# The last MLP chunk of a two-layer hybrid decoder: weight sums of two products built in a dead buffer, and the seven products in another order

## The chip, the cores and the metric

The kernel runs on one core of a Trainium2 chip. The metric is the device time of one execution in microseconds (us), lower is better. TensorE (PE) multiplies, VectorE (DVE), ScalarE (ACT) and GpSimd (POOL) work on elements, SyncE (SP) and GpSimd issue most DMA transfers. Each engine runs its own program in order; semaphores tie them together.

## The reference

Two layers, each with two token mixers merged by gates and then an MLP, on a sequence of 512 tokens and a width of 1024, all in float32. The change touches the MLP alone:

```
D_MODEL = 1024
SEQ = 512
DEPTH = 2
D_FF = 4 * D_MODEL
...
    h2 = rmsnorm(x, g_ffn)
    x = x + jnp.square(jax.nn.relu(h2 @ w_up)) @ w_down
```

## The kernel before

**Float32 in three passes.** Each float32 operand is split in a high part (a cast) and a low part (operand minus high part), and each product is three matmuls: high by high, high by low, low by high. ScalarE makes `w_hi`, DVE makes `w_lo`, both in two halves of 1024 columns; the same for the activations, `a_hi` and `a_lo`, of 128 x 1024 elements.

**The MLP by chunks.** The hidden width of 4096 is cut in `CH` = 4 chunks of 1024. For each chunk c, four up units `("U", c, u)` make the squared ReLU in the buffer `us[c % 2]`, and a down step multiplies it (512 x 1024) by 1024 x 1024 of `w_down`. The down step is done with seven products of halves in place of eight (Strassen's method in Winograd's form), numbered 1 to 7. Each product is a half of the tokens by a half of the chunk by a half of the output: 24 matmuls of 128 x 128 by 128 x 512 into two banks of PSUM. `M_SEQ` is the order of all units of the MLP; up units of the next chunk stand between the down products of a chunk, but the seven of the last chunk (`DOWN_LAST`, order 1 2 5 3 6 7 4) stand alone.

**Weight operands of the products.** With w00, w01, w10, w11 for the four quarters (h, m) of the chunk's `w_down`, product 1 uses w00, 5 uses w00+w01, 6 uses w00+w01+w11, 4 uses w00+w01+w11+w10, 3 uses w11, 7 uses w11+w01, and 2 uses w10. The sums are made by DMA: `sum_slot` (SP, L645) loads a quarter of 1 MB plain into `gh[slot]`, and `add_quarter` (GpSimd, L1114) adds another quarter to it with an accumulating DMA. Of the two buffers `gh`, one holds in turn the operands of 1, 5, 6, 4 (three adds) and the other those of 3, 7 (one add); which is which changes with the chunk. In the last chunk slot 1 has 1, 5, 6, 4 and slot 0 has 3, 7. Each add waits (`lo_done`) until DVE has read the operand that it overwrites. Product 2 reads w10 from the buffer `w_raw`, which all other weights pass through too (`load`, L475); a load waits until DVE's `w_lo` has read what was there.

**Activation operands.** Products 1, 2, 4 read a quarter of `us`, the others a sum: `sum_of` on DVE, in the chain 5, 6, 3 (each from the one before), and 7 by itself, in two buffers (`hn` and `sq`). `a_high` and `a_low` make the parts, in three sets that rotate.

**Order on the engines.** A weight set (two of them, rotating) is written once the product two before has been done (`mm_done`); so ScalarE's `weights_high` and DVE's `weights_low` work one unit ahead, in the order of `M_SEQ`, and an operand that isn't there yet holds up all that follow on ScalarE and DVE. TensorE starts a product when `a_ready`, the first half of `lo_done` and the eviction of the bank it needs (`acc_done`, `down_ready`) are there. Products 6, 7 and 4 are added in PSUM onto the bank that 1 opened, 3 onto that of 5; after each product DVE adds or subtracts the bank to the accumulators (`evict`), two of which are `acc[0]` and `tables`. In the last chunk all products are `halved`: the first 256 x 512 bank is finished, then the second (`down_halves`, `evict_half`), and each has its own eviction.

In layer 0 the last product is followed by transposes and the next layer's norm, in layer 1 by the final norm (`f_squares`, `f_scaled`) and the output. Both layers run the same down steps.

The functions that the change touches, with what calls them:

## Time and profile before

| | us |
|---|---|
| median of 3 runs | 1888.55 (1887.93 to 1889.95) |
| the profiled execution | 1888.48 |
| its span | 1886.4 |
| PE busy in the span | 1865.5 (99%) |
| DVE busy | 1255.6 (67%) |
| ACT busy | 837.2 (44%) |
| POOL busy | 129.4 (7%) |

The profile is of one execution. The span goes from its first to its last instruction. PE busy is modelled from the starts of pipelined matmuls; a matmul of 512 columns is shown with 0.39 us, but the next one starts 0.227 us after it, and this pace is what counts. Busy shares are means over the whole span; a gap on an engine is read in the timeline, where a row shows how long the engine had been idle and who released it. In the granted clock 1.00 is full speed (2.4 GHz). Layer 0's MLP ends near 941, layer 1's near 1879.

### The profile page before, as it was taken

To read this page: it belongs to the slowest core of one execution; us is meant where nothing else is said; L and a number is where in the kernel's file an instruction comes from. 1 tells how busy PE (TensorE), PEld (TensorE's weight loads), DVE (VectorE), ACT (ScalarE), POOL (GpSimd) and SP (SyncE) were. 2 spreads that over 40 slices of the span, in tenths; PEclk is the share of its full clock that TensorE was granted. 3 is DMA by queue.
4 is the path that set the end of the run, shared out by engine and by line. 5 is a ranking of instruction groups with operands and counts; after the bars stand their busy time and mean duration, and the time that the engine had idled before them with its cause. 6 is when DMAs were issued, how large, how long until landed. Compare 5 with 4: busy or idle time off the path is not lost.

```text
span 1886.4 us, 22990 instructions
## 1 busy us (share of the span) xinstructions
PE 1865.5 (99%) x9064; PEld 1549.7 (82%) x9064; DVE 1255.6 (67%) x1858; ACT 837.2 (44%) x1234; POOL 129.4 (7%) x104
## 2 busy tenths in 40 slices
PE   9999999999999999999899999999999999999997
PEld 7888888887888888888788888888878888888886
DVE  5356778767456666767863568788665575676777
ACT  7325465464223333434472255554632233344344
POOL 0001111100000000000000112111000000000100
PEclk9999999999999999999999999999999999999999
DMA  4543233333333465564626333233243334655655
GB/s 146 200 159 120 83 89 118 90 93 104 120 101 114 132 134 136 150 136 125 145 88 240 96 104 104 77 118 104 68 146 101 101 112 113 141 148 134 134 147 121
DMA packets 208235, 230.64 MB, mean 122 GB/s; under 512 B 13440, under 2 KB 160640, under 8 KB 207360
## 3 DMA queue, kind: packets, MB, share of 16 engines
q1 hardware_dynamic: 190512, 194.74, 32.7%
q0 software_dynamic: 16896, 33.56, 10.5%
q8 instruction: 72, 1.18, 0.2%
q10 hardware_dynamic: 720, 0.87, 0.1%
q14 instruction: 35, 0.29, 0.0%
HBM read 215.38 MB, written 13.77 MB: 121 GB/s over the span
## 4 chain that ended last, share of the span: by engine, by line
PE 85%; issue 6%; DVE 4%; DMA 3%; ACT 2%; POOL 0%; SPq 0%; POOLq 0%; ACTq 0%; DVEq 0%
PE pj L1816 19%; PE pj L1818 19%; PE pj L1817 19%; DMA gh<-in_w_down 2%; PE yr L2122 1%; PE yr L2124 1%; PE yr L2126 1%; DVE w_lo L1140 1%; PE pt L2122 1%; PE pt L2124 1%; PE pt L2126 1%; PE sc L2122 1%; PE sc L2124 1%; PE sc L2126 1%; PE yr L1923 1%
## 5 line engine op out<-in xcount | busy, mean ns | idle before, releaser
L1816 PE MATMUL pj<-h_hi,w_hi 128*128 128x512 f32 x1408 | 554.4, 394 | 1.0 <-DVE sA L1515 1.0
L1818 PE MATMUL pj<-h_hi,w_lo 128*128 128x512 f32 x1408 | 548.5, 390 | 0.0
L1817 PE MATMUL pj<-h_lo,w_hi 128*128 128x512 f32 x1408 | 548.3, 389 | 0.0
L1140 DVE TENSOR_TENSOR w_lo<-w_raw,w_hi 128x1024 fp32r<-128x1024 f32 x279 | 329.9, 1220 | 115.1 <-ACT w_hi L687 113.6
L687 ACT CAST w_hi<-w_raw 128x1024 fp32r<-128x1024 f32 x276 | 278.6, 1049 | 270.5 <-PE pj L1818 56.9
L1816 PEld LDWEIGHTS pj<-h_hi,w_hi 128*128 128x128 f32 x1408 | 264.4, 188 | 59.0 <-issue 1.9
L1818 PEld LDWEIGHTS pj<-h_hi,w_lo 128*128 128x128 f32 x1408 | 264.3, 188 | 56.0
L1817 PEld LDWEIGHTS pj<-h_lo,w_hi 128*128 128x128 f32 x1408 | 264.5, 188 | 53.9 <-issue 0.5
L697 ACT CAST w_hi<-gh 128x1024 fp32r<-128x1024 f32 x96 | 96.0, 1050 | 118.2 <-DMA gh<-in_w_down 50.5
L1107 POOL TENSOR_TENSOR rcos<-rot,tables 128x512 f32<-128x512 f32 x64 | 87.6, 1370 | 692.4 <-ACT rot L808 633.8
L1140 DVE TENSOR_TENSOR w_lo<-gh,w_hi 128x1024 fp32r<-128x1024 f32 x96 | 113.1, 1219 | 14.2 <-ACT w_hi L697 14.0
L975 ACT ACTIVATE relu<-pj 128x512 f32<-128x512 f32 x64 | 38.2, 597 | 189.6 <-PE pj L1818 189.6
L1581 DVE TENSOR_TENSOR u<-relu,rstd_all 128x512 f32<-128x512 f32 x64 | 44.0, 688 | 105.5 <-ACT relu L975 105.5
L1114 POOL DMA_DIRECT2D gh<-in_w_down x32 | 41.2, 1286 | 1038.4 <-DVE w_lo L1140 1038.4
L808 ACT COPY rot<-pj 128x512 f32<-128x512 f32 x48 | 27.9, 582 | 110.5 <-PE pj L1818 64.5
L2122 PE MATMUL sc<-w_hi,a_hi 128*128 128x512 f32 x160 | 63.3, 396 | 5.7 <-DVE a_lo L1623 3.4
L1288 DVE TENSOR_TENSOR swp<-swp,tables 128x512 f32<-128x512 f32 x64 | 65.4, 1022 | 4.4 <-ACT swp L812 2.7
L2126 PE MATMUL sc<-w_hi,a_lo 128*128 128x512 f32 x160 | 63.0, 394 | 0.0
L2124 PE MATMUL sc<-w_lo,a_hi 128*128 128x512 f32 x160 | 62.9, 393 | 0.0
L2122 PE MATMUL yr<-w_hi,a_hi 128*128 128x512 f32 x160 | 62.2, 389 | 0.0
L2124 PE MATMUL yr<-w_lo,a_hi 128*128 128x512 f32 x160 | 62.2, 389 | 0.0
L2126 PE MATMUL yr<-w_hi,a_lo 128*128 128x512 f32 x160 | 62.2, 389 | 0.0
(339 smaller groups left out, 3102.4 us busy)
## 6 DMA issues: line engine op xcount, KB each, us to landing
w_raw<-in_w_in SPq DMA_DIRECT2D x151, 512.0 KB, 4.7
w_raw<-in_w_up SPq DMA_DIRECT2D x64, 512.0 KB, 4.9
gh<-in_w_down POOLq DMA_DIRECT2D x32, 1024.0 KB, 8.7
gh<-in_w_down SPq DMA_DIRECT2D x16, 1024.0 KB, 5.1
w_raw<-in_w_b SPq DMA_DIRECT2D x16, 512.0 KB, 3.9
w_raw<-in_w_o SPq DMA_DIRECT2D x16, 512.0 KB, 3.9
w_raw<-in_w_down SPq DMA_DIRECT2D x16, 512.0 KB, 4.5
x_scratch<-x SPq DMA_DIRECT2D x2, 2048.0 KB, 10.1
```

What stands on the lines that cost most here:

```text
L687: nc.scalar.copy(w_hi[s][:, c], raw[:, c]).then_inc(hi_done, 1)
L697: nc.scalar.copy(w_hi[n % 2][:, h], gh[slot][:, h]).then_inc(hi_done, 1)
L1107: nc.gpsimd.tensor_tensor(rcos[:], rot[:], cosA if u < 3 else cosR, ALU.mult).then_inc(rot_cos, 1)
L1140: nc.vector.tensor_tensor(w_lo[s][:, c], src[:, c], w_hi[s][:, c], ALU.subtract).then_inc(lo_done, 1)
L1288: nc.vector.tensor_tensor(swp[:], swp[:], sinA if u < GROUPS else sinR, ALU.mult).then_inc(rot_sin, 1)
L1581: nc.vector.tensor_tensor(to, relu[:, o, :], rstd_all[:], ALU.mult).then_inc(relu_scaled, 1)
L1816: nc.tensor.matmul(out, w_hi[s][:, wc], acts[0], start=first, stop=False)
L1817: nc.tensor.matmul(out, w_hi[s][:, wc], acts[1], start=False, stop=False)
L1818: return nc.tensor.matmul(out, w_lo[s][:, wc], acts[0], start=False, stop=last)
L2122: nc.tensor.matmul(out, hi[:, k, t], w_hi[s][:, w], start=opens and k == 0, stop=False, skip_group_check=not opens)
L2124: nc.tensor.matmul(out, hi[:, k, t], w_lo[s][:, w], start=False, stop=False, skip_group_check=not opens)
L2126: return nc.tensor.matmul(out, lo[:, k, t], w_hi[s][:, w], start=False, stop=k == 3, skip_group_check=not opens)
```

## The change

Four things change, all in the last chunk (c = 3) of each layer:

1. The order of the seven products becomes 1 5 2 6 3 7 4, and the activation parts are made one product ahead in that order (`LAST_AHEAD`).
2. Product 1 reads w00 through `w_raw` (`plain`), with a load of its own on SP. `gh[1]` is still loaded with w00, but w01 is added at once, for product 5, and then w11 for product 6; `gh[0]` holds w11 for product 3 alone.
3. The operands of products 7 and 4 are built in `spares`, the two halves of `us[0]`, which held chunk 2's activations and is dead once `a_low` of (2,4) has read it. SP waits for that (`a_ready`) and loads w11 for 7 and w00 for 4; GpSimd adds one quarter for 7 and three for 4, each of these after the one before has landed.
4. Products 1, 5, 2, 6 and 3 are done whole and evicted whole; only 7 and 4 are still in halves.

GpSimd's last adds of layer 1 stand in its queue like this before (`gh_95` is slot 0, `gh_96` slot 1; `gh_96 x2` are the adds for products 5 and 6, the two after it those for 7 and 4):

```order
93 L1114 DMA gh_95<-in_w_down 128x4x512 [waits sum_in0,lo_done] x2
94 L1114 DMA gh_96<-in_w_down 128x4x512 [waits sum_in1,lo_done]
95 L1114 DMA gh_95<-in_w_down 128x4x512 [waits sum_in0,lo_done]
96 L1114 DMA gh_96<-in_w_down 128x4x512 [waits sum_in1,lo_done] x2
97 L1114 DMA gh_95<-in_w_down 128x4x512 [waits sum_in0,lo_done]
98 L1114 DMA gh_96<-in_w_down 128x4x512 [waits sum_in1,lo_done]
```

and now (`u_86` is `us[0]`):

```order
97 L1136 DMA gh_95<-in_w_down 128x4x512 [waits sum_in0,lo_done]
98 L1136 DMA gh_96<-in_w_down 128x4x512 [waits sum_in1]
99 L1144 DMA u_86<-in_w_down 128x4x512 [waits spare_in4]
100 L1144 DMA u_86<-in_w_down 128x4x512 [waits spare_in7]
101 L1144 DMA u_86<-in_w_down 128x4x512 [waits spare_added4] x2
102 L1136 DMA gh_96<-in_w_down 128x4x512 [waits sum_in1,lo_done]
```

The add for product 5 (row 98) no longer waits for `lo_done`; the four adds to the spares stand between it and the add for product 6 (row 102).

SP's last loads of weights in layer 1, before:

```order
191 L475 DMA w_raw<-in_w_up 128x4x256 [waits lo_done] x6
192 L645 DMA gh_96<-in_w_down 128x4x512 [waits lo_done]
193 L475 DMA w_raw<-in_w_down 128x2x512 [waits lo_done] x2
194 L645 DMA gh_95<-in_w_down 128x4x512 [waits lo_done]
195 L475 DMA w_raw<-in_w_down 128x2x512 [waits lo_done] x2
```

and now:

```order
193 L486 DMA w_raw<-in_w_up 128x4x256 [waits lo_done] x6
194 L656 DMA gh_96<-in_w_down 128x4x512 [waits lo_done]
195 L486 DMA w_raw<-in_w_down 128x2x512 [waits lo_done] x4
196 L679 DMA u_86<-in_w_down 128x4x512 [waits a_ready]
197 L679 DMA u_86<-in_w_down 128x4x512
198 L656 DMA gh_95<-in_w_down 128x4x512 [waits lo_done]
199 L486 DMA w_raw<-in_w_down 128x2x512 [waits lo_done] x2
```

Product 1's load (two of the x4) and the two loads of the spares are new, ahead of slot 0's load and of product 2's.

The diff, without the shorter pieces that only pass on the new order or the new test of `halved`:

```diff
-    DOWN_LAST = (1, 2, 5, 3, 6, 7, 4)
+    DOWN_LAST = (1, 5, 2, 6, 3, 7, 4)
+    LAST_AHEAD = {1: 2, 5: 6, 2: 3, 6: 7, 3: 4}
...
+    def plain(c, i):
+        return i == 2 or (c, i) == (CH - 1, 1)
+
     def by_raw(j):
-        return j < M0 or M_SEQ[j - M0][0] == "U" or M_SEQ[j - M0][2] == 2
+        return j < M0 or M_SEQ[j - M0][0] == "U" or plain(*M_SEQ[j - M0][1:])
...
-    def halved(c):
-        return c == CH - 1
+    def halved(c, i):
+        return c == CH - 1 and i in (7, 4)
...
+        spare = us[(CH - 2) % 2]
+        spares = {7: spare[:, 0:4, :].rearrange("p k c -> p (k c)"), 4: spare[:, 4:8, :].rearrange("p k c -> p (k c)")}
...
-                    load(m_unit(l, "D", c, 2), quarter(c))
+                    load(m_unit(l, "D", c, 2), quarter(c, 1))
+                    if c == CH - 2:
+                        load(m_unit(l, "D", c + 1, 1), quarter(c + 1, 0))
+                        sp.wait_ge(a_ready, l * LD + d_no(c, 4) + 1)
+                        for i, src in ((7, w_down_q[l, c + 1, 1, 1]), (4, w_down_q[l, c + 1, 0, 0])):
+                            sp.dma_start(spares[i].rearrange("p (k c) -> p k c", k=4), src).then_inc(spare_in[i], 16)
...
             def hi_sum(l, c, i, n):
+                if c == CH - 1 and i in (7, 4):
+                    act.wait_ge(spare_added[i], (l + 1) * 16 * {7: 1, 4: 3}[i])
+                    for h in HALVES:
+                        nc.scalar.copy(w_hi[n % 2][:, h], spares[i][:, h]).then_inc(hi_done, 1)
+                    return
...
                 def add_quarter(c, behind, as_sum, h, m):
                     slot = slot_of(l, c, as_sum)
-                    pool.wait_ge(lo_done, m_unit(l, "D", c, behind) * 2 + 2 + UNIT_CREDIT)
+                    if not plain(c, behind):
+                        pool.wait_ge(lo_done, m_unit(l, "D", c, behind) * 2 + 2 + UNIT_CREDIT)
                     pool.wait_ge(sum_in[slot], (l * CH + c) * 16 + 16)
...
+                def add_spare(i, n, h, m):
+                    if n == 0:
+                        pool.wait_ge(spare_in[i], l * 16 + 16)
+                    else:
+                        pool.wait_ge(spare_added[i], (l * 3 + n) * 16)
+                    nc.gpsimd.dma_start(spares[i].rearrange("p (k c) -> p k c", k=4), w_down_q[l, CH - 1, h, m],
+                                        accum_op=ALU.add).then_inc(spare_added[i], 16)
+
-                for c in range(CH):
+                for c in range(CH - 1):
                     add_quarter(c, 1, True, 0, 1)
                     add_quarter(c, 5, True, 1, 1)
                     add_quarter(c, 3, False, 0, 1)
                     add_quarter(c, 6, True, 1, 0)
+                add_quarter(CH - 1, 1, True, 0, 1)
+                add_spare(4, 0, 0, 1)
+                add_spare(7, 0, 0, 1)
+                add_spare(4, 1, 1, 1)
+                add_spare(4, 2, 1, 0)
+                add_quarter(CH - 1, 5, True, 1, 1)
...
-                    if last_chunk and i == 2:
-                        sum_of(c, 3)
...
                     if (kind, c, i) == ("D", CH - 2, 4):
-                        a_low(CH - 1, 2)
+                        a_low(CH - 1, 5)
                         sum_of(CH - 1, 6)
                     if last_chunk:
-                        for t in {1: (5,), 2: (3,), 5: (6,), 3: (7,), 6: (4,)}.get(i, ()):
-                            a_low(c, t)
-                        if i != 4:
+                        if i == 7:
                             evict_half(i, 0)
-                        if i == 5:
-                            sum_of(c, 7)
+                        if i in LAST_AHEAD:
+                            a_low(c, LAST_AHEAD[i])
+                        if i in (5, 2):
+                            sum_of(c, {5: 3, 2: 7}[i])
```

## Rows read from the trace of the kernel before

**Rows 1.** PE's waits, whole span: releaser: us in total, times, longest.

```profile
PE sc L2122 <- DVE a_lo L1623: 3.4, 2, 1.9
PE pt L2122 <- DVE a_lo L1623: 3.1, 2, 1.7
PE sc L2122 <- DVE tables L1647: 2.3, 2, 1.5
```

**Rows 2.** Timeline of PE, last chunk of both layers: start, us, [idle before <-releaser].

```profile
896.21 0.39 PE L2122 MATMUL sc<-w_hi,a_hi 128*128 128x512 f32 x1
...
938.86 0.48 PE L2122 MATMUL sc<-w_hi,a_hi 128*128 128x512 f32 x1
...
941.45 0.39 PE L2126 MATMUL sc<-w_hi,a_lo 128*128 128x512 f32 x1
...
1834.79 0.39 PE L2122 MATMUL sc<-w_hi,a_hi 128*128 128x512 f32 x1
...
1852.64 0.47 PE L2122 MATMUL pt<-w_hi,a_hi 128*128 128x512 f32 x1 [1.37 <-DVE a_lo L1623]
...
1879.19 0.39 PE L2126 MATMUL sc<-w_hi,a_lo 128*128 128x512 f32 x1
```

**Rows 3.** Busy time by stretch; PEclk is the third number from the end.

```profile
907.00:925.00 18.00, 16.28 (x73) 13.15 (x72) 15.77 (x17) 9.16 (x10) 3.87 (x3) 1.00 0.79 132
1866.00:1869.50 3.50, 3.50 (x10) 2.76 (x9) 0.62 (x2) 1.34 (x2) 0.00 (x0) 0.52 0.44 81
```

**Rows 4.** Timeline of ACT in layer 1's last chunk.

```profile
1836.58 1.05 ACT L687 CAST w_hi<-w_raw 128x1024 fp32r<-128x1024 f32 x1 [0.35 <-DMA w_raw<-in_w_down]
...
1842.57 2.00 ACT L697 CAST w_hi<-gh 128x1024 fp32r<-128x1024 f32 x2 [3.99 <-DMA gh<-in_w_down]
...
1855.34 2.00 ACT L697 CAST w_hi<-gh 128x1024 fp32r<-128x1024 f32 x2 [6.52 <-DMA gh<-in_w_down]
...
1860.39 2.00 ACT L697 CAST w_hi<-gh 128x1024 fp32r<-128x1024 f32 x2 [2.09 <-DMA gh<-in_w_down]
```

**Rows 5.** Timeline of POOL, layer 1's last adds.

```profile
1790.65 1.28 POOL L1114 DMA_DIRECT2D gh<-in_w_down  x1 [9.23 <-DVE w_lo L1140]
1833.39 1.28 POOL L1114 DMA_DIRECT2D gh<-in_w_down  x1 [41.46 <-DVE w_lo L1140]
1846.53 1.28 POOL L1114 DMA_DIRECT2D gh<-in_w_down  x1 [11.85 <-DVE w_lo L1140]
1851.11 1.28 POOL L1114 DMA_DIRECT2D gh<-in_w_down  x1 [3.30 <-DVE w_lo L1140]
```

**Rows 6.** Line 1114 from 1859 to 1860, one add, from issue to landing.

```profile
DMA to landing us min/median/max: 8.6/8.6/8.6
```

**Rows 7.** Timeline of DVE in both layers.

```profile
879.90 2.35 DVE L1623 TENSOR_TENSOR a_lo<-u,a_hi 128x1024 fp32r<-128x1024 f32 x2
...
1818.95 2.35 DVE L1623 TENSOR_TENSOR a_lo<-u,a_hi 128x1024 fp32r<-128x1024 f32 x2
...
1830.75 2.35 DVE L1140 TENSOR_TENSOR w_lo<-gh,w_hi 128x1024 fp32r<-128x1024 f32 x2
...
1850.73 1.22 DVE L1623 TENSOR_TENSOR a_lo<-hn,a_hi 128x1024 fp32r<-128x1024 f32 x1
```

**Rows 8.** The chain that ended last, one piece: start, us, what.

```profile
1801.63 5.11 DMA gh<-in_w_down
```

**Rows 9.** Timeline of SP's DMA queue in layer 1.

```profile
1793.91 1.66 SPq L475 DMA_DIRECT2D w_raw<-in_w_up  x2
...
1811.01 1.50 SPq L475 DMA_DIRECT2D w_raw<-in_w_down  x2
1828.46 0.37 SPq L645 DMA_DIRECT2D gh<-in_w_down  x1
1828.87 1.02 SPq L475 DMA_DIRECT2D w_raw<-in_w_down  x2
```

**Rows 10.** Busy time by stretch; the last two numbers are DMA share and GB/s.

```profile
1812.00:1813.00 1.00, 1.00 (x6) 0.84 (x5) 0.11 (x1) 0.00 (x0) 0.00 (x0) 1.00 0.87 152
1850.00:1859.00 9.00, 7.63 (x34) 6.02 (x33) 6.85 (x8) 2.95 (x3) 1.28 (x1) 1.00 1.11 202
```

**Rows 11.** DMA queues, 1794.9 to 1797: the only queue with packets.

```profile
q0 software_dynamic: 205, 0.42, 111.4%
```

More of the change, by code:

```diff
@@ L126, in slot_of, with adds_of @@
         return (l * CH + c) % 2 if as_sum else 1 - (l * CH + c) % 2
+    def adds_of(c, as_sum):
+        return (2 if as_sum else 0) if c == CH - 1 else (3 if as_sum else 1)
     def adds_before(l, c, as_sum):
-        w, s = l * CH + c, slot_of(l, c, as_sum)
-        return w // 2 * 4 + ((3 if s == 0 else 1) if w % 2 else 0)
+        slot = slot_of(l, c, as_sum)
+        return sum(adds_of(w % CH, slot_of(0, w, True) == slot) for w in range(l * CH + c))
     with ExitStack() as ctx:
@@ L396, in trunk @@
         sum_added = [sem(f"sum_added{i}") for i in range(2)]
+        spare_in = {i: sem(f"spare_in{i}") for i in (7, 4)}
+        spare_added = {i: sem(f"spare_added{i}") for i in (7, 4)}
         a_sum = sem("a_sum")
@@ L633, in _, with quarter @@
                         load(l * LU + O0 + i * O_U + u, cols(w_o_u[l], 2 * i + u))
-                def quarter(c):
+                def quarter(c, h):
                     d = raw[:].rearrange("p (k c) -> p k c", k=4)
-                    return [(d[:, m:m + 2, :], w_down_q[l, c, 1, 0][:, m:m + 2, :]) for m in (0, 2)]
+                    return [(d[:, m:m + 2, :], w_down_q[l, c, h, 0][:, m:m + 2, :]) for m in (0, 2)]
                 def sum_slot(c, as_sum):
@@ L993, in weights_high @@
                         kind, c, i = M_SEQ[j]
-                        if kind == "D" and i != 2:
+                        if kind == "D" and not plain(c, i):
                             hi_sum(l, c, i, n)
@@ L1056, in _ @@
                     if (kind, c, i) == ("D", CH - 2, 4):
-                        a_high(CH - 1, 2)
+                        a_high(CH - 1, 5)
                     if kind == "D" and c == CH - 1:
-                        for t in {1: (5,), 2: (3,), 5: (6,), 3: (7,), 6: (4,)}.get(i, ()):
-                            a_high(c, t)
+                        if i in LAST_AHEAD:
+                            a_high(c, LAST_AHEAD[i])
                         if last_layer and i == 7:
-                            f_squares(0, (0, 1), 2 * d_no(c, 6) + 2)
-                            f_squares(1, (0, 1), 2 * d_no(c, 6) + 2)
+                            f_squares(0, (0, 1), 2 * d_no(c, 3) + 2)
+                            f_squares(1, (0, 1), 2 * d_no(c, 3) + 2)
                             f_root(0, 2)
@@ L1588, in weights_low @@
                         kind, c, i = M_SEQ[j]
-                        if kind == "D" and i != 2:
+                        if kind == "D" and not plain(c, i):
                             for hf in range(2):
-                                lo_half(n, n % 2, hf, gh[slot_of(l, c, i in (1, 5, 6, 4))])
+                                lo_half(n, n % 2, hf, spares[i] if c == CH - 1 and i in (7, 4) else
+                                        gh[slot_of(l, c, i in (1, 5, 6, 4))])
                             return
@@ L1673, in _ @@
                             relu_square(before[1], before[2], 1)
-                        elif before[1] == CH - 1:
+                        elif halved(*before[1:]):
                             evict_half(before[2], 1)
@@ L1698, in _ @@
                     if (kind, c, i) == ("D", CH - 2, 4):
-                        a_low(CH - 1, 2)
+                        a_low(CH - 1, 5)
                         sum_of(CH - 1, 6)
                     if last_chunk:
-                        for t in {1: (5,), 2: (3,), 5: (6,), 3: (7,), 6: (4,)}.get(i, ()):
-                            a_low(c, t)
-                        if i != 4:
+                        if i == 7:
                             evict_half(i, 0)
-                        if i == 5:
-                            sum_of(c, 7)
+                        if i in LAST_AHEAD:
+                            a_low(c, LAST_AHEAD[i])
+                        if i in (5, 2):
+                            sum_of(c, {5: 3, 2: 7}[i])
                     if kind == "U":
@@ L2130, in down_ready @@
                     held = {1: (c - 1, 2), 6: (c, 1), 7: (c, 6), 4: (c, 7), 5: (c - 1, 3), 3: (c, 5), 2: (c - 1, 4)}[i]
-                    if b == 0 or not halved(c):
+                    if b == 0 or not halved(c, i):
                         pe.wait_ge(a_ready, l * LD + d_no(c, i) + 1)
                     if held[0] >= 0:
-                        pe.wait_ge(acc_done, l * LA + 2 * d_no(*held) + 1 + (b if halved(held[0]) else 1))
+                        pe.wait_ge(acc_done, l * LA + 2 * d_no(*held) + 1 + (b if halved(*held) else 1))
                     elif l == DEPTH - 1:
@@ L2190, in _ @@
                             gains_spread()
-                    elif halved(c):
+                    elif halved(c, i):
                         down_halves(c, i)
```

## The prediction

> **What bounds the kernel now.** I read the page first: TensorE is busy 99% of the span, so nothing but TensorE's own work or a gap on it can move the time. Then TensorE's waits: all its gaps that another engine causes in the MLP are three kinds of two [rows 1], 8.8 us together, and all six lie in the last MLP chunk, three in each of the two layers. The timeline says where. In layer 1 the seven products of that chunk begin at 1834.79 and the last matmul begins at 1879.19, 44.6 us with its own 0.23 us [rows 2]; at the pace of the other products (24 matmuls of 0.227 us, 5.44 us, for each) they would take 38.1. The missing 6.5 us are the gaps (1.4 us idle before product 3, 1.9 before product 7, 0.8 inside product 4, each some 0.15 us longer by starts) and a slow stretch: after the 1.9 us gap the granted clock falls to 0.52 of full over 3.5 us, that is to the lower of its two levels (1.2 GHz) [rows 3], and product 7 takes 7.1 us in place of 5.44, 1.7 us lost. In layer 0 the chunk runs from 896.21 to 941.45 [rows 2], 45.5 us with the last matmul, of which 1.7 go to transposes between the halves of product 4 (from the end of the half at 937.20 to 938.86 [rows 2]); 5.7 us are missing there, and the clock stays at 1.00 over that stretch [rows 3].
>
> Why those gaps: ScalarE's casts of the weight sums wait for the accumulating DMA of `gh`, by 2 to 6.5 us [rows 4], and so DVE's `w_lo` and `a_lo` are late. Each add costs an issue of 1.28 us on GpSimd [rows 5] and lands 8.6 us after the issue began when it has the queue for itself [rows 6]; slot 1 has three of them in a row, and each waits until the sum before it has been read. So the whole that the change can win is what is missing: 6.5 in layer 1 and 5.7 in layer 0.
>
> **The change, part by part.** Bytes and casts first. TensorE's 168 matmuls a chunk stay. ScalarE and DVE cast and subtract as often. A whole eviction is one DVE operation on 1024 columns, 1.22 us like the others of that size [rows 7], and lies beside matmuls: zero on the path. DVE's fullest products are 5 and 2, each with an eviction, two halves of `w_lo`, an `a_lo` and a `sum_of`, 5 x 1.2 = 6.0 us in 5.44; the 0.6 too much is given back in the products around them. The moved `sum_of` and `a_low` calls feed the new order one product ahead: zero as well. What costs is DMA: seven plain or accumulating transfers of 1 MB in the chunk (raw weights of product 2 counted) become twelve, and six of them accumulate where four did.
>
> What becomes early: product 1 reads a plain load, so the sum for product 5 need not wait for product 1. It is issued as soon as `gh` has landed, at 1806.8 (the load at 1801.63 took 5.1 us [rows 8]) where it now waits until 1833.39 [rows 5]. Product 3 reads slot 0 as loaded. The sum of product 7 is one add in a buffer of its own.
>
> What becomes late is the sum of **product 6**, now fourth and due at 1834.79 + 3 x 5.44 = 1851.1. Its add waits for nothing new in data, but stands last in GpSimd's queue, behind product 4's three adds, of which the second and third each wait for the one before to land. GpSimd holds the program there. I work out when it gets through, in layer 1.
>
> 1. The spare loads. They wait for `a_ready` of (2,4), the first of the two `a_lo` at 1818.95, done near 1820.1 [rows 7]. The add for product 5 now transfers from about 1809 to 1814 and meets the plain load for product 2 of chunk 2, issued at 1811.01 [rows 9]; I put 0.8 us of delay on it, so the spare loads are issued at about 1821. How long 2 MB of plain loads take: the `gh` load at 1828.46 and the two halves behind it [rows 9] were awaited until 1836.58 [rows 4], 8.1 us. So the second one, for product 4, lands at **1829.0** (the plain load of product 1, issued at 1818.5 to 1819.8, lies ahead of them and is nearly through).
> 2. Product 4's first add is issued at 1829.0 and lands 8.6 us later [rows 6], at 1837.6.
> 3. Product 7's add is issued 1.3 us behind it. Two adds at once don't go twice as fast: those issued at 1846.53 and 1851.11 landed at 1855.3 and 1860.4, 5.1 us apart [rows 4, 5], and in that stretch the DMA engines were full at 202 GB/s [rows 10], which is 1 MB in 5.2 us. So it lands at 1842.7.
> 4. Product 4's second add, issued at 1837.7, comes behind it: 1847.8. Its third is issued at 1847.9 and lands at 1856.5.
> 5. Product 6's add is issued at 1849.2 and lands 5.1 us after that, **1861.6**.
> 6. From landing to matmul: half a cast (1.05), half a `w_lo` (1.22), and 0.7 from DVE's end to TensorE's start (the `a_lo` that began at 1850.73 ended at 1851.95, and the matmul began at 1852.64 [rows 2, 7]): 3.0. Product 6 starts at 1864.6, **13.5 us late**.
>
> A second wait hides in front of it. Product 2's plain load can be issued only when product 1's `w_lo` has read `w_raw`, at 1832 to 1833.1 [rows 7]. By then the adds are transferring. The plain load issued at 1793.91 [rows 9], in the middle of the add of 1790.65 [rows 5], moved nothing until the add was nearly over: from 1794.9 to 1797 only the accumulating queue has packets [rows 11], though the plain load of 1811.01 had filled the engines by 1812 to 1813 [rows 10]. So product 2's load sits until product 4's second add has ended, some 0.6 us before its landing, near 1847, gets the pause of about 3 us until the third one starts, and lands at 1849 to 1850. Product 2, due at 1845.7, starts near 1852 and ends at 1857.4, before 1864.6: this wait is inside the 13.5.
>
> Here the Trainium skill says otherwise (DMA: Bandwidth & Descriptors, Queues, rings and completion order): a DMA engine takes turns between the rows that have work, packet by packet. The rows just read don't look like turns. By that rule product 2's load would be in time and product 4's adds later; this is a rival below.
>
> The sum. Layer 1 then misses 13.5, plus the slow clock after so long a gap (1.7, as it cost behind the gap before product 7 [rows 3]; what falls between products 2 and 6 is covered by the wait), plus 0.4 left inside product 4: 15.6 in place of 6.5, +9.1. In layer 0 the `a_lo` of (2,4) began at 879.90 [rows 7], 16.3 us ahead of product 1 where it is 15.8 in layer 1, so the wait is 13.0; with 1.7 and 0.5 it is 15.2 in place of 5.7, +9.5. After the chunk everything is as before and moves along. 1888.48 (the profiled execution) + 18.6 = 1907.1; the median of the runs, 1888.55, is the same within 0.1. **Forecast 1907.**
>
> Ends of the unknown costs. If the spare loads land 1.5 us sooner, product 7's add costs product 4's nothing, and the clock costs nothing, each layer is 1.5 + 1.3 + 1.7 = 4.5 us better: 1898. If the spare loads land 1.5 us later: 1910.
>
> **The rivals.** (a) Product 2's second half misses the pause. The pause is about 3 us and 1 MB needs 2.6 us at the fastest; one slow engine, and the load waits until product 6's add has landed. ScalarE casts in order, so product 2's half, its cast, `w_lo`, the rest of the product and DVE's row up to `w_lo` of product 6 follow one another, and product 6 starts at about 1870, 5.4 us later. One layer gives 1912, both 1918. For it: the pause is tight. Against: the plain load behind the add of 1790.65 was through soon after it.
>
> (b) The two queues take turns. The mechanism here: product 2's load takes 2.6 us of the engines between 1833 and 1838, the adds behind it shift by that, and product 6 starts at 1867.2. 2.6 more in each layer: 1912. Against it is the empty plain queue in [rows 11]. This is what the rule of the Trainium skill named above would do.
>
> (c) The adds run side by side at full speed. Then product 6's add is issued at 1829.0 + 2 x 8.6 + 1.3 = 1847.6 and lands at 1856.2, product 6 starts at 1859.2, 8.1 us late: about 5 us better in each layer, 1896. The full engines of [rows 10] and the 5.1 us between landings speak against it.
>
> (d) The other side: the wait for product 6's sum is not there, and the change wins what it is after. That needs the add landed by 1851.1 - 3.0 = 1848.1, so the spare loads landed about 13 us earlier than I have them, near 1816, before `a_lo` of (2,4) is done. If I have misread what GpSimd stands behind, the gaps and the slow clock go but for 0.4 us in each layer: 1888.5 - 11.3 = 1877. For it: five of the seven products do get their weights well ahead.
>
> **How the numbers follow.** The forecast as worked out 0.60; (a) 0.18; (b) 0.08; (c) 0.08; (d) 0.06. A measurement here tells about 0.2%, 3.8 us, from no change. Faster is (d), 0.06. The same: (c) with an early spare load, 0.03. Slower: 0.91. The range takes in the forecast's own ends, 1898 to 1910, and most of (a), (b) and (c): 1896 to 1917.
>
> **What would show it.** In the profile after: TensorE has in each layer one wait before product 2 and one before product 6, 6 to 7 us each (product 2 stands between them), 13 us late in all, with a clock of 0.5 after them. GpSimd's last add of a layer is issued 14.4 us after product 1 starts, and product 4's adds 8.6, then 10, then 10 us apart, landing to landing. ScalarE waits for `gh` before product 6 and nowhere behind it. The gaps before 3 and 7 and most of that inside 4 are gone. Wrong would be: the last add issued before 1840 on layer 1's scale (then (d)), landings of adds less than 5 us apart (then (c)), or plain packets among accumulating ones (then (b)).

## The result, and the profile after

The changed kernel takes **1924.38 us** (median of 4 runs, 1923.79 to 1925.47). The kernel before takes 1888.24 in the same comparison (4 runs, 1887.38 to 1889.95). The ratio is 1.0191, 95% interval 1.0173 to 1.0209: slower by 36 us. The forecast was 1907 with a range to 1917, so the direction is right, and the slowdown is nearly twice what was forecast (36 us where 18.6 were).

The profiled execution took 1923.79, its span 1922.0. TensorE is as busy as before, 1866.2 us, but that is 97% of the span where it was 99%. TensorE's largest wait on another engine (releaser: us in total, times, longest) is one row in place of [rows 1], and one small one is left in the chunk:

```profile
PE sc L2157 <- DVE w_lo L1176: 43.0, 2, 22.7
PE sc L2157 <- DVE tables L1684: 0.3, 1, 0.3
```

The timeline of PE puts it in both layers, before product 6, as [rows 2] did for the gaps of before (first matmul of the chunk, first matmul of product 6, last matmul; for layer 0 and layer 1):

```profile
896.32 0.39 PE L2157 MATMUL sc<-w_hi,a_hi 128*128 128x512 f32 x1
...
935.54 0.77 PE L2157 MATMUL sc<-w_hi,a_hi 128*128 128x512 f32 x1 [22.73 <-DVE w_lo L1176]
...
960.70 0.39 PE L2161 MATMUL sc<-w_hi,a_lo 128*128 128x512 f32 x1
...
1853.79 0.39 PE L2157 MATMUL sc<-w_hi,a_hi 128*128 128x512 f32 x1
...
1890.54 0.76 PE L2157 MATMUL sc<-w_hi,a_hi 128*128 128x512 f32 x1 [20.27 <-DVE w_lo L1176]
...
1914.82 0.39 PE L2161 MATMUL sc<-w_hi,a_lo 128*128 128x512 f32 x1
```

Products 1, 5 and 2 run at full pace, and product 6 is due 3 x 5.44 = 16.3 us after product 1 starts: at 912.64 and 1870.11. It starts 22.9 and 20.4 us late. Behind it nothing waits but 0.3 us. In layer 1 the chunk takes 1853.79 to 1914.82 and 0.23, 61.3 us; 23.2 are missing against the pace of 38.1, where 6.5 were. In layer 0 it is 64.6, less 1.7 of transposes, and 24.9 are missing, where 5.7 were. Together 16.7 + 19.1 = 35.8 us, within 0.5 us of the whole difference (35.3 us between the two profiled executions, 36.1 between the medians).

After the wait the clock stands at its lower level, as it did behind the 1.9 us gap in [rows 3] (busy time by stretch, the granted clock third from the end):

```profile
1890.00:1894.00 4.00, 3.46 (x8) 2.81 (x9) 4.00 (x5) 3.04 (x5) 0.00 (x0) 0.50 0.00 0
```

Product 6 takes 7.6 us in place of 5.44 in layer 1: 2.2 lost, and 1.9 in layer 0.

Where product 6's sum was, GpSimd's timeline shows, in layer 1 and then layer 0 (L1136 is the add to `gh` for product 6, L1144 are those to the spares; of the x2 the first is product 4's first, the second product 7's). Compare [rows 5]:

```profile
1851.45 2.62 POOL L1144 DMA_DIRECT2D u<-in_w_down  x2 [24.21 <-DMA u<-in_w_down]
1864.03 1.28 POOL L1144 DMA_DIRECT2D u<-in_w_down  x1 [9.96 <-DMA u<-in_w_down]
1874.12 1.28 POOL L1144 DMA_DIRECT2D u<-in_w_down  x1 [8.80 <-DMA u<-in_w_down]
1874.87 1.84 POOL L1136 DMA_DIRECT2D gh<-in_w_down  x1
...
893.89 2.59 POOL L1144 DMA_DIRECT2D u<-in_w_down  x2 [23.87 <-DMA u<-in_w_down]
906.63 1.30 POOL L1144 DMA_DIRECT2D u<-in_w_down  x1 [10.15 <-DMA u<-in_w_down]
919.52 1.29 POOL L1144 DMA_DIRECT2D u<-in_w_down  x1 [11.59 <-DMA u<-in_w_down]
920.27 1.85 POOL L1136 DMA_DIRECT2D gh<-in_w_down  x1
```

The add for product 6 is the last row of each. In layer 1 it is issued 21.1 us after product 1 starts, and ScalarE, which casts in order, stands still until it lands, at 1888.09. Before that ScalarE cast the weights of product 2. The first row is the second half of that cast, the second row is product 6's (compare [rows 4]):

```profile
1861.26 1.06 ACT L703 CAST w_hi<-w_raw 128x1024 fp32r<-128x1024 f32 x1 [0.77 <-DMA w_raw<-in_w_down]
...
1888.09 1.99 ACT L718 CAST w_hi<-gh 128x1024 fp32r<-128x1024 f32 x2 [24.83 <-DMA gh<-in_w_down]
```

and SP's queue had issued its loads so (compare [rows 9]; the x4 are the loads of product 2 of chunk 2 and of product 1 of chunk 3, L679 the spares, L656 slot 0, the last x2 product 2):

```profile
1830.00 10.09 SPq L486 DMA_DIRECT2D w_raw<-in_w_down  x4
1840.86 0.92 SPq L679 DMA_DIRECT2D u<-in_w_down  x2
1847.46 0.37 SPq L656 DMA_DIRECT2D gh<-in_w_down  x1
1850.99 1.50 SPq L486 DMA_DIRECT2D w_raw<-in_w_down  x2
```

One row already speaks against the forecast: product 2's weights were cast at 1861.26, while the adds of 1851.45 were still transferring. TensorE had no wait there: product 2 was not late at all. Its load had been issued at 1850.99, 0.5 us ahead of product 4's first add, and not 3 us behind it as forecast.

### The profile page after: what moved, and what is told of

Its sections match the earlier page's. It is cut to its first block, busy times and chain, and to the rows that moved or that the text cites. A ratio compares the mean times of both kernels' runs of the same rounds, so it can differ in the third digit from the quotient of the medians.

```text
span 1922.0 us, 22976 instructions
## 1 busy us (share of the span) xinstructions
PE 1866.2 (97%) x9064; PEld 1551.0 (81%) x9064; DVE 1255.4 (65%) x1848; ACT 837.4 (44%) x1234; POOL 134.2 (7%) x108
## 4 chain that ended last, share of the span: by engine, by line
PE 87%; DMA 5%; DVE 3%; ACT 2%; issue 2%; POOL 0%; SPq 0%; ACTq 0%; DVEq 0%; POOLq 0%
PE pj L1851 19%; PE pj L1853 19%; PE pj L1852 19%; DMA u<-in_w_down 2%; PE sc L2157 1%; PE sc L2159 1%; PE sc L2161 1%; PE yr L2157 1%; PE yr L2159 1%; PE yr L2161 1%; DMA gh<-in_w_down 1%; PE pt L2161 1%; PE pt L2159 1%; PE pt L2157 1%; DVE w_lo L1176 1%
## 5 line engine op out<-in xcount | busy, mean ns | idle before, releaser
L1176 DVE TENSOR_TENSOR w_lo<-w_raw,w_hi 128x1024 fp32r<-128x1024 f32 x283 | 334.9, 1220 | 120.6 <-ACT w_hi L703 119.3
L703 ACT CAST w_hi<-w_raw 128x1024 fp32r<-128x1024 f32 x280 | 282.9, 1050 | 280.3 <-PE pj L1853 56.9
L718 ACT CAST w_hi<-gh 128x1024 fp32r<-128x1024 f32 x84 | 83.9, 1049 | 133.4 <-DMA gh<-in_w_down 72.3
L1176 DVE TENSOR_TENSOR w_lo<-gh,w_hi 128x1024 fp32r<-128x1024 f32 x84 | 99.0, 1221 | 48.0 <-ACT w_hi L718 47.7
L1136 POOL DMA_DIRECT2D gh<-in_w_down x28 | 37.1, 1325 | 941.7 <-DVE w_lo L1176 911.4
L2157 PEld LDWEIGHTS sc<-w_hi,a_hi 128*128 128x128 f32 x160 | 31.0, 194 | 51.0 <-issue 43.8
## 6 DMA issues: line engine op xcount, KB each, us to landing
u<-in_w_down POOLq DMA_DIRECT2D x8, 1024.0 KB, 12.3
```

The source lines that it names most:

```text
L703: nc.scalar.copy(w_hi[s][:, c], raw[:, c]).then_inc(hi_done, 1)
L718: nc.scalar.copy(w_hi[n % 2][:, h], gh[slot][:, h]).then_inc(hi_done, 1)
L1176: nc.vector.tensor_tensor(w_lo[s][:, c], src[:, c], w_hi[s][:, c], ALU.subtract).then_inc(lo_done, 1)
L2157: nc.tensor.matmul(out, hi[:, k, t], w_hi[s][:, w], start=opens and k == 0, stop=False, skip_group_check=not opens)
```

## The experiments

The theory after this result: (Q) product 6's add stands in GpSimd's queue behind adds that wait for each other, and the forecast undersized how long these take; the size comes from plain loads that share the DMA engines with the adds (this is T, which alone would hold product 6 back wherever its add stands). The rivals: something else holds product 6 back (its own data, ScalarE's or DVE's order); or plain loads do stand still while adds transfer, and the adds are slow for another cause. Times below are medians; the kernel before took 1886.4 to 1888.7 in these comparisons.

**Product 6's add first.** On the changed kernel, in GpSimd's program:

```diff
                 add_quarter(CH - 1, 1, True, 0, 1)
+                add_quarter(CH - 1, 5, True, 1, 1)
                 add_spare(4, 0, 0, 1)
                 add_spare(7, 0, 0, 1)
                 add_spare(4, 1, 1, 1)
                 add_spare(4, 2, 1, 0)
-                add_quarter(CH - 1, 5, True, 1, 1)
```

> The changed kernel with one line moved: in GpSimd's queue the add for product 6 stands directly behind the add for product 5, ahead of all four adds to the spare buffer. Times on the scale of the changed kernel's layer 1 (product 1 starts at 1853.8, product 6 is due at 1870.1). Theory Q (the position in GpSimd's queue made the wait): the add for 6 is issued near 1852 when DVE has read product 5's sum, lands near 1862.5, and product 6 starts on time; product 4's three adds end near 1886, so product 4 starts some 3 us late. Time near 1883. Rival T (too much DMA traffic, wherever the add stands): product 6 still starts more than 10 us late, time above 1905.

Measured: 1901.54, ratio to the kernel before 1.0076 (1.0060 to 1.0092), 23 us faster than the changed kernel. One line moved, and product 6 starts on time in both layers. In its place TensorE waits before product 4, 9.8 us in layer 0 and 9.5 us in layer 1, and 1.2 us before product 7 in layer 0:

```profile
PE sc L2157 <- DVE tables L1684: 19.2, 2, 9.8
```

```profile
1846.83 1.30 POOL L1136 DMA_DIRECT2D gh<-in_w_down  x1 [31.14 <-DVE w_lo L1176]
1847.59 3.17 POOL L1144 DMA_DIRECT2D u<-in_w_down  x2
1860.98 1.28 POOL L1144 DMA_DIRECT2D u<-in_w_down  x1 [10.22 <-DMA u<-in_w_down]
1871.63 1.28 POOL L1144 DMA_DIRECT2D u<-in_w_down  x1 [9.37 <-DMA u<-in_w_down]
```

(TensorE's waits, then GpSimd's timeline; the first row is the add for product 6.) So the place in the queue is the mechanism. The price was expected too small: product 4 was to start some 3 us late, and the time was to be near 1883. Its three serial adds need more than 30 us, from 1847.59 until its cast at 1880.41, and here they begin behind product 6's add. The last product becomes late in its turn.

**Product 6's add in the middle**, between product 7's and product 4's second:

```diff
                 add_spare(4, 0, 0, 1)
                 add_spare(7, 0, 0, 1)
+                add_quarter(CH - 1, 5, True, 1, 1)
                 add_spare(4, 1, 1, 1)
                 add_spare(4, 2, 1, 0)
-                add_quarter(CH - 1, 5, True, 1, 1)
```

> The changed kernel with the add for product 6 behind the first adds for 4 and 7, but ahead of 4's second and third. Theory Q with adds served one after another at 5.1 us each: its add is issued near 1854 and lands near 1872.5 (layer 1 of the changed kernel), product 6 starts 5 to 6 us late and pays the slow clock (2 us), nothing else waits. Time near 1892. Theory T: about as the changed kernel, above 1905. If two adds ran side by side at full speed it would land near 1866 and the time would be 1880.

Measured: 1899.91 (one run). Product 6 waits 8.9 us in layer 0 and 5.6 in layer 1. Its add was issued at 1848.39 and its cast began at 1863.58, 15.2 us later, for two adds issued at 1841.18 were ahead of it:

```profile
1841.18 2.62 POOL L1144 DMA_DIRECT2D u<-in_w_down  x2 [23.74 <-DMA u<-in_w_down]
1848.39 1.28 POOL L1136 DMA_DIRECT2D gh<-in_w_down  x1 [4.59 <-DVE w_lo L1176]
```

Both places for product 6's add leave the kernel 12.5 to 14.2 us slower than it was before the change: with the four adds to the spares one product or another is late. The next version takes three of the four out.

**A separate sum for product 7 alone; product 4 goes on from product 6's sum.** On the changed kernel; product 4 then reads `gh[1]` after one more add (w10), as before the change:

```diff
-                        for i, src in ((7, w_down_q[l, c + 1, 1, 1]), (4, w_down_q[l, c + 1, 0, 0])):
+                        for i, src in ((7, w_down_q[l, c + 1, 1, 1]),):
...
                 add_quarter(CH - 1, 1, True, 0, 1)
-                add_spare(4, 0, 0, 1)
                 add_spare(7, 0, 0, 1)
-                add_spare(4, 1, 1, 1)
-                add_spare(4, 2, 1, 0)
                 add_quarter(CH - 1, 5, True, 1, 1)
+                add_quarter(CH - 1, 6, True, 1, 0)
```

> Part of the change: new order, product 1 by a plain load, but only product 7 is built in the spare buffer. Product 4 uses product 6's sum plus one quarter, so its sum is product 6's slot with one more add, as in the kernel before. Adds in the chunk: four again, for 5, 7, 6, 4 in this order in GpSimd's queue. Theory Q: no add waits for another that has nothing to do with it; each lands at least 3 us before its product is due; the gaps of the kernel before and its slow clock are gone. Time 1876 to 1879, faster than before by 0.5 to 0.6%. Theory T (the plain loads added for product 1 and the spare buffer are what costs): product 6 starts 2 us or more late, time 1885 or more.

Measured: **1876.56** (1876.3 to 1878.69, 5 runs), ratio 0.9944 (0.9931 to 0.9957). It beats both kernels. PE, first and last matmul of layer 1's chunk, and the busy time of the chunk (clock third from the end):

```profile
1831.30 0.39 PE L2155 MATMUL sc<-w_hi,a_hi 128*128 128x512 f32 x1
...
1869.71 0.39 PE L2159 MATMUL sc<-w_hi,a_lo 128*128 128x512 f32 x1
```

```profile
1831.30:1870.00 38.70, 38.44 (x169) 31.27 (x167) 34.66 (x36) 23.72 (x36) 2.58 (x2) 1.00 0.57 128
```

The chunk takes 38.64 us against the pace of 38.08, at full clock: of the missing time of [rows 1, 3] all but 0.6 is won in this layer. The adds now stand apart from each other. Product 6's cast still waits for its add, early enough that TensorE does not wait; the casts of products 7 and 4 find their data there (released by TensorE, not by a DMA):

```profile
1825.81 1.28 POOL L1144 DMA_DIRECT2D u<-in_w_down  x1 [21.10 <-DMA u<-in_w_down]
1835.58 1.28 POOL L1136 DMA_DIRECT2D gh<-in_w_down  x1 [8.49 <-DVE w_lo L1174]
1848.56 1.30 POOL L1136 DMA_DIRECT2D gh<-in_w_down  x1 [11.69 <-DVE w_lo L1174]
```

```profile
1844.44 2.00 ACT L718 CAST w_hi<-gh 128x1024 fp32r<-128x1024 f32 x2 [3.09 <-DMA gh<-in_w_down]
...
1853.26 2.00 ACT L709 CAST w_hi<-u 128x1024 fp32r<-128x1024 f32 x2 [1.97 <-PE sc L2159]
...
1858.70 2.01 ACT L718 CAST w_hi<-gh 128x1024 fp32r<-128x1024 f32 x2 [2.48 <-PE pt L2159]
```

(GpSimd, then ScalarE: products 6, 7 and 4.)

**The order alone, without a spare buffer.** On the changed kernel; 5, 6, 4 in slot 1 and 3, 7 in slot 0, as before the change, in the new order:

```diff
                 add_quarter(CH - 1, 1, True, 0, 1)
-                add_spare(4, 0, 0, 1)
-                add_spare(7, 0, 0, 1)
-                add_spare(4, 1, 1, 1)
-                add_spare(4, 2, 1, 0)
                 add_quarter(CH - 1, 5, True, 1, 1)
+                add_quarter(CH - 1, 3, False, 0, 1)
+                add_quarter(CH - 1, 6, True, 1, 0)
```

> Parts 1, 2 and 4 of the change without the spare buffer: order 1 5 2 6 3 7 4, product 1 by a plain load, sums 5, 6, 4 in slot 1 and 3, 7 in slot 0, in GpSimd's queue 5, 6, 7, 4. Only product 7 can be late: its add can start when product 3's operand has been read, about 6 us before 7 is due, and takes 8.7. Theory Q: product 7 starts some 5 us late in each layer with a slow clock behind it (2 us), nothing else waits. Time near 1891. If the new order alone were worth anything beside the sums it would be below 1885.

Measured: 1894.79 (5 runs), ratio 1.0034 (1.0022 to 1.0046). The wait is before product 7, 6.8 and 5.8 us, since its add can only be issued when product 3's operand has been read. So the order and the plain load of product 1 alone don't win; with the spare for product 7 they do.

**2 MB of plain loads beside an add.** This and the next take the kernel before and add two loads of 1 MB into the dead buffer `us[0]`, whose data nobody reads. Here they are issued when product 5's operand has been read, which is when the add for product 6 is issued:

```diff
+                sp.wait_ge(lo_done, m_unit(l, "D", CH - 1, 5) * 2 + 2 + UNIT_CREDIT)
+                for q in range(2):
+                    sp.dma_start(us[0][:, 4 * q:4 * q + 4, :], w_down_q[l, CH - 1, q, 0]).then_inc(extra_in, 16)
```

> The kernel before with 2 MB of plain loads more in each layer, into the buffer that is dead there, issued by SP at the moment at which GpSimd issues the add for product 6 (both wait for product 5's low part). Nothing reads them. If the DMA engines serve what came first (a plain load starts about 1 us sooner than an accumulating one), no accumulating packets move until the plain ones are through: the add lands 5 us later (near 13.5 us after its issue in place of 8.7), and product 6 starts about 4 us late. If they take turns, packets of both queues move together from the start, and the plain loads take about as long as the add. Time by both near 1896 to 1900; the packets by queue tell them apart.

Measured: 1899.2 (one run). The add issued at 1853.05 is cast at 1866.03, 13.0 us later; in the kernel before the same add took 8.8, from 1846.53 to the cast at 1855.34 [rows 4, 5]. Product 6 waits 6.4 and 3.6 us. The DMA queues from 1859 to 1863 (packets, MB, share of 16 engines):

```profile
q0 software_dynamic: 264, 0.54, 73.2%
q1 hardware_dynamic: 233, 0.45, 35.4%
```

In this stretch the accumulating queue (q0) and the plain queue (q1) move nearly as many packets. Before it the plain queue moved nearly alone: the add's first packets came 4.8 us after its issue, where they come 2.0 us after it when nothing else transfers.

**The plain loads inside a train of adds.** The order of arrival is turned round: the loads are issued while product 6's add transfers, as in [rows 11], and 0.3 us ahead of product 7's add.

```diff
+                sp.wait_ge(lo_done, m_unit(l, "D", CH - 1, 3) * 2 + 2 + UNIT_CREDIT)
+                for q in range(2):
+                    sp.dma_start(us[0][:, 4 * q:4 * q + 4, :], w_down_q[l, CH - 1, q, 0]).then_inc(extra_in, 16)
```

> The kernel before with 2 MB of plain loads more in each layer into the dead buffer, issued when product 3's operand has been read, that is at the issue of product 7's add and some 4.5 us after that of product 6's add, so in the middle of 10 us of accumulating. Nothing reads them. My forecast's reading (a plain load gets nothing while adds transfer): no plain packets until both adds are through, and the add for 7 lands 9.2 us after its issue as before. Turns, after a wait of about 3 us behind what the other queue has already fetched: plain packets appear some 4 us after the issue, next to accumulating ones and as many as they, and the add for 7 lands 3 to 4 us later than before, product 7 starts as much later, time near 1896.

Measured: 1898.97 (one run). SP's issue, and the queues from 1865 to 1869:

```profile
1855.72 1.58 SPq L671 DMA_DIRECT2D u<-in_w_down  x2
```

```profile
q0 software_dynamic: 255, 0.52, 70.1%
q1 hardware_dynamic: 256, 0.52, 39.1%
```

The plain queue has its first packets at about 1858.8, 3.1 us after the issue, when product 6's add is nearly through. Then it moves nearly alone until product 7's add has its first packets at about 1861.9, 5.9 us after its issue. The queues from 1859 to 1862:

```profile
q1 hardware_dynamic: 428, 0.88, 95.7%
q0 software_dynamic: 18, 0.01, 2.6%
```

From 1863 to 1870 the two move packet for packet, and the add issued at 1855.98 lands after 15.0 us where it took 9.2. This decides against a step of the forecast: plain loads don't stand still for as long as adds transfer, and the adds pay for them. The 2.1 us without a plain packet in [rows 11] lie inside a late start: that load had its first packets at about 1797.5, 3.6 us after its issue.

**Whole or half products.** The best kernel with all seven products in halves again:

```diff
     def halved(c, i):
-        return c == CH - 1 and i in (7, 4)
+        return c == CH - 1
```

> The kernel of e4_chain_564 with all seven products in halves, each with two half evictions, in place of whole ones for 1, 5, 2, 6, 3. Shows what the whole reads are worth once no sum is late. By the rows of DVE a pair of half evictions costs 0.25 us more than a whole one, and all of it lies beside TensorE's work: the same as e4_chain_564 within 1 us. If DVE's row decides (6 us of work in a product of 5.44), it is 1 to 3 us slower.

Measured: 1878.38 (1877.4 to 1881.39, 5 runs), ratio 0.9946 (0.9934 to 0.9959) where whole reads had 0.9944. The intervals overlap: whole reads are worth nothing that can be measured.

**The old order with the rest.** The best kernel's separate sum and plain product 1, but the order and the halves of before:

```diff
-    DOWN_LAST = (1, 5, 2, 6, 3, 7, 4)
+    DOWN_LAST = (1, 2, 5, 3, 6, 7, 4)
```

> The kernel before with its own order 1 2 5 3 6 7 4 and its halves, and only the DMA part of e4_chain_564: product 1 by a plain load, so that the add for 5 is early, and product 7's sum in the spare buffer. Theory: what made the gaps of the kernel before is the landing of sums alone, so this is worth as much as e4_chain_564, 1876 to 1879. The new order is then not needed. If the order matters: product 2's plain load, which now waits until product 1's has been read, comes 1 to 2 us late in each layer, 1879 to 1882.

Measured: 1896.9 (5 runs), ratio 1.0043 (1.0029 to 1.0057). The expectation missed. Both products 1 and 2 now read through `w_raw`, one right after the other, so product 2's load is issued only when product 1's weights have been read; product 7's add, issued at 1833.17, is then under way. Product 2 is 4 us late in both layers, with smaller gaps behind it:

```profile
PE yr L2147 <- DVE w_lo L1165: 7.8, 2, 4.0
```

This is the case that the forecast had in mind, a plain load issued behind an add that is under way (in layer 1 at 1835.66). It has its first packets at about 1839.5, 3.8 us later, when the add has moved about half of its 512 packets. From then on the queues move alike, from 1840 to 1843:

```profile
q0 software_dynamic: 183, 0.37, 68.0%
q1 hardware_dynamic: 185, 0.38, 38.7%
```

So the load begins late and then takes turns with the add; it doesn't wait for the add's end. And the new order, with product 5 between the two plain products, is a needed part of the win.

**What lengthens product 4's first add.** In the changed kernel it took 12.3 us to land where [rows 6] had 8.6, and GpSimd issued the next one 12.6 us after it; the times below are from issue to next issue. Three candidates were beside it: slot 0's load, product 7's add, product 2's load. First without slot 0's load (product 3 then reads what was in the buffer):

```diff
+                    if c == CH - 1 and not as_sum:
+                        sp.sem_inc(sum_in[slot], 16)
+                        return
```

> The changed kernel without the 1 MB plain load of slot 0 in the last chunk (product 3 reads what was there, so its part of the result is not the reference's). Prices one megabyte of plain load that lies between the spare loads and product 4's first add. With turns between the queues and a rate of 2.6 us for a plain megabyte: the first add lands 2 to 3 us sooner (9.5 to 10 us after its issue in place of 12.3) and product 6 starts 2 to 3 us sooner in each layer, time 1924.4 - 5 = 1919. If plain loads did not slow adds (my forecast): no change, 1924.

Measured: 1926.54 (2 runs), ratio 1.0207 (1.0177 to 1.0237): no gain. The add still took 12.1 us in layer 1, so it is not that load. Then without product 7's add (product 7 then uses w11 alone):

```diff
-                add_spare(7, 0, 0, 1)
```

> The changed kernel without the add for product 7 (product 7 uses w11 alone, so its part of the result is not the reference's). Prices step 3 of the forecast: adds share one rate. Product 4's second add then does not come behind another: it lands 8.6 us after its issue in place of 9.8 to 12.6. Everything behind it is 1.3 us sooner in layer 1, a little more in layer 0, and product 4's chain otherwise unchanged: time 1920 to 1922. If each add cost its full 5.1 us on the path: 1914.

Measured: 1918.79 (2 runs), ratio 1.0166 (1.0136 to 1.0195). That is 5.6 us less than the changed kernel, somewhat more than the 2.4 to 4.4 expected. The first add still takes 12.3 us (1848.31 to 1860.58), the second now 8.7:

```profile
1848.31 1.28 POOL L1147 DMA_DIRECT2D u<-in_w_down  x1 [24.65 <-DMA u<-in_w_down]
1860.58 1.30 POOL L1147 DMA_DIRECT2D u<-in_w_down  x1 [10.99 <-DMA u<-in_w_down]
1869.30 1.29 POOL L1147 DMA_DIRECT2D u<-in_w_down  x1 [7.42 <-DMA u<-in_w_down]
```

So the second add's 10.1 us came from product 7's add ahead of it. Last, product 2's load held back until the first add has landed:

```diff
+                    if c == CH - 1:
+                        sp.wait_ge(spare_added[4], l * 48 + 16)
                     load(m_unit(l, "D", c, 2), quarter(c, 1))
```

> The changed kernel with one wait more: SP issues product 2's plain load only when product 4's first add has landed. Tests what lengthened that add (12.3 us from issue to landing, where it takes 8.6 alone), now that the run without slot 0's load left it at 12.1. If it is product 2's load, issued 0.5 us ahead of it: the first add lands 8.6 to 9 us after its issue. Product 2's load then meets product 4's second add or product 7's and lands about 6 to 8 us after its issue, so product 2 is some 5 us late, inside the wait for product 6. Product 6 starts 1 to 3 us sooner after product 1 than in the changed kernel (36.75 us in layer 1). If the first add still takes 12 us, it is something else, as the add for product 7 issued right behind it.

Measured: 1924.84 (one run). The first add takes 8.6 us, but now the second takes 13.7:

```profile
1852.19 2.62 POOL L1146 DMA_DIRECT2D u<-in_w_down  x2 [24.09 <-DMA u<-in_w_down]
1860.76 1.28 POOL L1146 DMA_DIRECT2D u<-in_w_down  x1 [5.95 <-DMA u<-in_w_down]
1874.48 1.28 POOL L1146 DMA_DIRECT2D u<-in_w_down  x1 [12.44 <-DMA u<-in_w_down]
```

So it was product 2's load that lengthened the first add, and holding it only moves the cost to the next one. Product 6 starts 36.4 us after product 1, 0.4 sooner and not the 1 to 3 expected. Product 2's load is here issued while adds transfer: its first packets came 4.0 us later, and product 2 started 4.5 us late. That is the first wait of the forecast, which the changed kernel didn't have.

How the load did it in the changed kernel is in the DMA queues of layer 1, from 1852 to 1856 and then from 1857 to 1861:

```profile
q1 hardware_dynamic: 491, 0.94, 82.8%
...
q0 software_dynamic: 384, 0.79, 107.3%
q1 hardware_dynamic: 37, 0.07, 5.1%
```

The plain packets went first. The add's own first packets came at about 1856.4, 5.0 us after its issue in place of 2.0, and there was little left to take turns with. This late start is 3.0 of the 3.7 us.

## Why the prediction was right in its direction and too small

Times of layer 1 in the changed kernel stand 19.0 us later than on the forecast's scale, by product 1's start.

**What bounds the kernel, and what can be won**: right. The forecast put it at 11.3 us and a kernel without those gaps at 1877; the version with one separate sum runs in 1876.56.

**The mechanism** (product 6's add last in GpSimd's queue, behind serial adds): right, shown by moving that one line. The gaps before products 3 and 7 went, as forecast; what is left inside product 4 is 0.4 us from start to start in layer 1 and nothing in layer 0.

**The steps**, in layer 1:

| step of the forecast | forecast | measured | miss |
|---|---|---|---|
| 1. spare loads issued | 1821 | 1840.86 - 19.0 = 1821.9 | +0.9 |
| 1. from there until the first add is issued | 8.1 | 10.6 | +2.5 |
| 2. first add lands after | 8.6 | 12.3 | +3.7 |
| 3, 4. second add to third | 10.2 | 10.1 | -0.1 |
| 5. third add's issue until product 6's cast | 13.7 | 14.0 | +0.3 |
| 6. landing to matmul | 3.0 | 2.5 | -0.5 |

These make 6.8 of the 6.9 us by which product 6 was later than forecast (20.4, not 13.5). Step 1 held product 1's 1 MB load for nearly through; SP had issued it just ahead of the spare loads, within the row of 1830.00, and 3 MB had to pass. Step 2 took the landing time of an add that has the queue for itself, though product 2's load is issued beside it, at 1850.99. That adds share one rate (step 3) held: without product 7's add the next one lands in 8.7 us.

In **layer 0** the same steps are late, and the second add takes 12.9 us in place of 10.2. The next layer's first weights are loaded beside it:

```profile
904.40 1.62 SPq L521 DMA_DIRECT2D w_raw<-in_w_in  x2
```

This load was not in the forecast, which scaled layer 0 from layer 1. It is the likeliest cause of the extra 2.7 us, but it was not tried by itself. In the kernel without product 7's add, with the same load beside it, the second add of layer 0 took 9.2 us, so the load alone doesn't account for the 2.7.

**The step that failed** is "A second wait hides in front of it": a plain load gets nothing while adds transfer, so it costs product 2 a hidden wait and the adds nothing. Two things in it were wrong.

- The adds do pay. Product 4's first add took 3.7 us longer to land than step 2 has it, and 8.6 us as forecast once product 2's load was held back. Beside 2 MB of plain loads two other adds took 4.2 and 5.8 us longer. The price was put on product 2, where it was covered; it falls on the adds, where each microsecond counts.
- The order was the other one. On the forecast's scale product 2's load was issued at 1832.0, as forecast, but product 4's first add at 1832.5 and not at 1829.0, since step 1 was 3.4 us too short. So the load went ahead of the adds, product 2 was in time, and layer 1 of the changed kernel has no load issued behind these adds. The kernels that have one (the loads inside a train of adds, the old order) show a late start and then equal packets.

So of the 6.9 us by which product 6 was later than forecast, 3.7 are this step's and 3.4 are step 1's, which held product 1's load for nearly through; the other steps all but cancel.

This comes nearest to rival (b), and the rule of the Trainium skill (DMA: Bandwidth & Descriptors, Queues, rings and completion order) that an engine takes turns between rows with work. The measurement agrees with it once both queues move, 255 packets to 256 in 4 us; the late start before that is not in it. The rival had 0.08, and its 2.6 us a layer was too small for the first add alone. Rival (a) fell with the same step, (c) by the 10.1 us from the second add to the third, of which product 7's add made 1.4, (d) by the result.

**The clock**: forecast 1.7 us in each layer, measured 2.2 and 1.9. Together, wait, clock and rest put layer 1 7.6 us and layer 0 9.6 us over the forecast, 17.2 in all: 1907.1 + 17.2 = 1924.3, where the profiled execution took 1923.79 and the median 1924.38.

## What to carry to other kernels

Transfers in one engine's program that wait for each other are a block for all behind them: put the one that is due first in front, or better, extend a chain that exists by one add than build the same sum anew with three. When a path runs through DMA, list every transfer issued while it runs, from every queue, and expect each to delay what is issued next to it. And a few microseconds in which a queue moves nothing may be only its late start; look further on before calling it blocked.

## What the runs showed of the hardware

- A queue that gets work while another is busy begins late. An add's first packets came 4.8, 5.0 and 5.9 us after its issue when plain loads were moving, 2.0 us alone. A plain load's came 3.1, 3.6, 3.8 and 4.0 us after its issue when an add was moving, 1.0 us alone. In three of these four the add was nearly through by then, in one (the old order) it was half done.
- Once both have begun, both move the same number of packets: 255 to 256 and 183 to 185. Until then one can have the engines nearly to itself: 428 to 18 in 3 us.
- An accumulating packet takes 1.8 times the time of a plain one of the same 2 KB (70.1% of the engines for 255 packets, 39.1% for 256), so by packets an equal turn is no equal share of time.
- After 20 us of idle TensorE's granted clock was 0.50 and product 6 took 7.6 us; after a gap of 1.9 us [rows 3] it had been 0.52 and product 7 took 7.1. Here a gap ten times as long cost only 0.5 us more in clock, and in layer 0, behind 22.7 us of idle, 1.9 us were lost.
